# A state-space stage in fp32 on one core: gated output kept in the squares buffer, and six small jobs of VectorE given to GpSimd

## The reference, cut to what matters

```
y = ssd_chunked_scan(x32 * dt[..., None], dt * a_cont, bmat, cmat)
y = y + d_skip[:, None] * x32
y = y.reshape(b, seq, D_INNER) * silu(z)
y = rmsnorm(y.reshape(b, seq, 4, 512), ssd_norm_w.reshape(4, 512))
y_ssd = y.reshape(b, seq, D_INNER) @ w_branch_ssd
# pooling, windows 2, 4, 8, 16
mean = (csg[:, 1:] - start) / minimum(count, float(win))
outs.append(mean - u[..., gi * gw:(gi + 1) * gw])
y_pool = (einsum('blgc,gcd->blgd', pooled, pool_w) * pool_scale) @ w_branch_pool
out = (g_ssd * y_ssd + g_pool * y_pool) @ w_out
```

## Time and profile before

| | |
|---|---|
| Median of 3 runs | 1147.05 us (1146.51 to 1148.46) |
| The profiled execution's own time | 1148.47 us |
| Its span, first to last instruction | 1146.7 us |
| Mean granted TensorE clock | 0.996 |

### The profile page before, as it was taken

One profiled execution on the slowest core, in us unless ns is written; L12 is line 12 of the kernel. 1 busy time (PEld: TensorE's weight loads), 2 busy tenths in 40 slices (PEclk: granted clock), 3 DMA queues, 4 the chain that ended last, 5 costly groups with the idle time before them and its releaser, 6 DMA issues.

```text
span 1146.7 us, 25636 instructions
## 1 busy us (share of the span) xinstructions
PE 1116.8 (97%) x9126; PEld 1076.4 (94%) x9126; DVE 978.8 (85%) x1785; ACT 711.4 (62%) x1109; POOL 34.7 (3%) x64
## 2 busy tenths in 40 slices
PE   8989999999999999999999999999999999999997
PEld 7989999999899999999999989999899999999997
DVE  7877999998998998989999889999997678766667
ACT  6557656666556556565666677878876457645554
POOL 0000000000000100000000000000000000000000
PEclk9999999999999999999999999999999999999999
DMA  8534676675566866856766537457546556665661
GB/s 289 177 119 155 210 238 233 221 262 186 192 251 258 308 225 245 302 198 238 237 209 212 183 101 255 146 202 155 186 155 232 174 197 217 214 198 199 200 202 38
DMA packets 73042, 235.73 MB, mean 206 GB/s; under 512 B 7425, under 2 KB 16641, under 8 KB 72849
## 3 DMA queue, kind: packets, MB, share of 16 engines
q1 hardware_dynamic: 64304, 203.86, 53.4%
q0 software_dynamic: 8528, 30.98, 7.9%
q10 hardware_dynamic: 144, 0.02, 0.0%
HBM read 233.73 MB, written 1.09 MB: 205 GB/s over the span
## 4 chain that ended last, share of the span: by engine, by line
PE 73%; DVE 17%; issue 4%; ACT 4%; DVEq 1%; DMA 1%; ACTq 0%; SPq 0%; another core or an unknown queue 0%
PE ps L248 22%; PE ps L250 21%; PE ps L249 21%; DVE w_lo L240 5%; PE ps L280 3%; PE ps L282 2%; DVE arena L2009 1%; ACT w_hi L235 1%; DVE arena L502 1%; DVE arena L939 1%; DMA w_raw<-stream 1%; DVE arena L1997 0%; PE ps L1674 0%; DVE arena L974 0%; ACT sq L421 0%
## 5 line engine op out<-in xcount | busy, mean ns | idle before, releaser
L240 DVE TENSOR_TENSOR w_lo<-w_raw,w_hi 128x1024 fp32r<-128x1024 f32 x381 | 461.1, 1218 | 11.1 <-ACT w_hi L235 5.1
L248 PE MATMUL ps<-a_hi,w_hi 128*128 128x256 f32 x1656 | 463.8, 280 | 4.8 <-DVE w_lo L240 3.2
L250 PE MATMUL ps<-a_hi,w_lo 128*128 128x256 f32 x1656 | 456.2, 276 | 0.0
L249 PE MATMUL ps<-a_lo,w_hi 128*128 128x256 f32 x1656 | 456.1, 275 | 0.0
L235 ACT ACTIVATE w_hi<-w_raw 128x1024 fp32r<-128x1024 f32 x381 | 390.7, 1049 | 20.9 <-DMA w_raw<-stream 11.8
L248 PEld LDWEIGHTS ps<-a_hi,w_hi 128*128 128x128 f32 x1656 | 318.5, 192 | 12.0 <-issue 5.5
L249 PEld LDWEIGHTS ps<-a_lo,w_hi 128*128 128x128 f32 x1656 | 318.5, 192 | 0.6 <-issue 0.2
L250 PEld LDWEIGHTS ps<-a_hi,w_lo 128*128 128x128 f32 x1656 | 318.7, 192 | 0.0
L248 PE MATMUL ps<-b_both,w_hi 128*128 128x256 f32 x560 | 155.7, 278 | 2.2 <-DVE b_both L999 1.3
L249 PE MATMUL ps<-b_both,w_hi 128*128 128x256 f32 x560 | 154.0, 275 | 0.0
L250 PE MATMUL ps<-b_both,w_lo 128*128 128x256 f32 x560 | 154.0, 275 | 0.0
(11 more groups left out here) (315 smaller groups left out, 1683.1 us busy)
## 6 DMA issues: line engine op xcount, KB each, us to landing
w_raw<-stream SPq DMA_DIRECT2D x381, 512.0 KB, 4.2
arena<-ada POOLq DMA_DIRECT2D x48, 512.0 KB, 5.9
c_both<-cum_rows POOLq DMA_DIRECT2D x4, 1024.0 KB, 8.7
arena<-x SPq DMA_DIRECT2D x2, 512.0 KB, 4.5
con<-consts SPq DMA_DIRECT2D x1, 1024.0 KB, 5.7
arena<-row_cols POOLq DMA_DIRECT2D x2, 512.0 KB, 5.2
arena<-c_rows POOLq DMA_DIRECT2D x1, 512.0 KB, 4.2
out<-arena SPq DMA_DIRECT2D x2, 256.0 KB, 2.2
```

The lines of the kernel that those rows point to most:

```text
L240: dve.tensor_tensor(w_lo[:, s % RING], w_raw[:, s % RING], w_hi[:, s % RING].bitcast(F32), ALU.subtract).then_inc(w_lo_ready, 1)
L248: pe.matmul(o, wh, xh, start=start, stop=False, skip_group_check=shared)
L249: pe.matmul(o, wh, xl, start=False, stop=False, skip_group_check=shared)
L250: return pe.matmul(o, wl, xh, start=False, stop=stop, skip_group_check=shared)
```

## The change

`y_f`, the gated `y`, now lies in `sq[:, 4:8]`. It is written there at j = 0 instead of `z_s` and scaled in place with tokens in order. The even and odd tokens are parted later, when ScalarE copies it to `b_hi` and when the low part is taken. GpSimd gets, in its one queue: for each group the two additions of squares and the low part of `y`, and the low parts of the four poolings (one instruction of 512 columns each instead of two of 256). VectorE waits for the low part of group g - 1 at j = 11 instead of ahead of `gaps(2)`, and from the second pooling on for the low part of the one before. The constant ones for the last pooling's scan move to `sq[:, 3]`, set at m = 5. For the first three groups GpSimd's work stands behind the DMA of the next group's `cum_all`.

```diff
@@ -80,6 +80,11 @@
     return x.rearrange("p m (a t) -> p m a t", a=2)
+def parted_four(x):
+    return x.rearrange("p m (t a) -> p m a t", a=2)
@@ -1530,7 +1535,7 @@
         y_seen = area(4 * SEQ + 2 * SEEN)
-        y_f = y_seen[:, 0:4 * SEQ].rearrange("p (a t) -> p a t", a=4)
+        y_f = sq[:, 4:8]
         seen = [y_seen[:, c:c + SEEN] for c in (4 * SEQ, 4 * SEQ + SEEN, 0, SEEN)]
@@ -1768,13 +1773,13 @@
                     act.wait_ge(yz_ready, in_group(1, 1, g, it))
-                    act.activation(sq[:, 0:4], z_s, ACT.Square).then_inc(ysq_ready, 1)
+                    act.activation(sq[:, 0:4], y_f, ACT.Square).then_inc(ysq_ready, 1)
                 if j == 3:
...
                     o = slice(4 * g, 4 * g + 4) if it is None else bass.ds(it * 4 + 4 * g, 4)
-                    act.activation(b_hi[:, o], y_f, ACT.Copy).then_inc(yhi_ready, 1)
+                    act.activation(halves_wide(b_hi[:, o]), parted_four(y_f), ACT.Copy).then_inc(yhi_ready, 1)
@@ -1903,6 +1908,24 @@
+        def ssd_pool(pool, g):
+            pool.wait_ge(ysq_ready, g + 1)
+            add_four(pool, ADDED_SSD + 2 * g, 2, None)
+            y_low(pool, g)
+        def pooled_lo(pool, g):
+            pool.wait_ge(pooled_hi, g + 1)
+            lo, hi = (halves_wide(x[:, 2 * g:2 * g + 2]) for x in (c_lo, c_hi))
+            pool.tensor_tensor(lo, parted_four(win_of(g)), hi.bitcast(F32), ALU.subtract).then_inc(pooled_operand, 1)
+        def y_low(pool, g):
+            pool.wait_ge(yhi_ready, g + 1)
+            y, hi, lo = parted_four(y_f), halves_wide(b_hi[:, 4 * g:4 * g + 4]), halves_wide(b_lo[:, 4 * g:4 * g + 4])
+            pool.tensor_tensor(lo, y, hi.bitcast(F32), ALU.subtract).then_inc(yssd_ready, 1)
         def win_of(g):
@@ -1958,22 +1981,15 @@
                     dve.wait_ge(z_silu, in_group(1, 1, g, it))
-                    dve.tensor_tensor(z_s, cv[:, 2:6], z_s, ALU.mult).then_inc(yz_ready, 1)
-                if j == 1:
-                    dve.wait_ge(ysq_ready, in_group(1, 1, g, it))
-                    add_four(dve, ADDED_SSD + 2 * g, 2, it)
+                    dve.tensor_tensor(y_f, cv[:, 2:6], z_s, ALU.mult).then_inc(yz_ready, 1)
                 if j == 3:
...
                     for t in range(4):
-                        ins = dve.scalar_tensor_tensor(out=halves(y_f[:, t]), in0=parted(z_s[:, t]), scalar=prm(34 + t, g, it), in1=parted(inv_s),
+                        ins = dve.scalar_tensor_tensor(out=y_f[:, t], in0=y_f[:, t], scalar=prm(34 + t, g, it), in1=inv_s,
                                                        op0=ALU.mult, op1=ALU.mult)
                     ins.then_inc(yn_ready, 1)
-                if j == 7:
-                    dve.wait_ge(yhi_ready, in_group(1, 1, g, it))
-                    o = slice(4 * g, 4 * g + 4) if it is None else bass.ds(it * 4 + 4 * g, 4)
-                    dve.tensor_tensor(b_lo[:, o], y_f, b_hi[:, o].bitcast(F32), ALU.subtract).then_inc(yssd_ready, 1)
@@ -1982,8 +1998,6 @@
                         dve.wait_ge(rows_landed, in_group(16, 16, g, it))
-                    if k == 2 and g:
-                        dve.wait_ge(yssd_ready, in_group(1, 1, g - 1, it))
                     if k >= 4:
@@ -1997,7 +2011,7 @@
                 for j in range(GRP):
-                    if g and j != 7:
+                    if g:
                         tail(j, g - 1, it)
@@ -2029,8 +2043,6 @@
                         weighted(0)
-                    if g and j == 7:
-                        tail(j, g - 1, it)
                     if j > 8:
@@ -2041,6 +2053,8 @@
                         gaps(3)
+                    if g and j == 11:
+                        dve.wait_ge(yssd_ready, in_group(1, 1, g - 1, it))
                     if j == 11:
@@ -2052,7 +2066,6 @@
             dve.wait_ge(u_done, 2 * GROUPS)
-            step(dve.memset(sq[:, NT - 1], 1.0))
@@ -2062,7 +2075,7 @@
                     for t in range(2):
-                        ins = dve.tensor_tensor_scan(running[:, t], sq[:, NT - 1], u[:, t], 0.0, ALU.mult, ALU.add)
+                        ins = dve.tensor_tensor_scan(running[:, t], sq[:, 3], u[:, t], 0.0, ALU.mult, ALU.add)
                     step(ins)
@@ -2078,13 +2091,6 @@
-            def pooled_lo(g):
-                dve.wait_ge(pooled_hi, g + 1)
-                for m in (2 * g, 2 * g + 1):
-                    ins = dve.tensor_tensor(halves(c_lo[:, m]), parted(win_of(g)[:, m % 2]), halves(c_hi[:, m].bitcast(F32)), ALU.subtract)
-                ins.then_inc(pooled_operand, 1)
-                dve.wait_ge(pooled_operand, g + 1)
             def pools():
@@ -2096,14 +2102,15 @@
                 tail(m, GROUPS - 1, None)
-                if m - 1 == POOL_AT[-1]:
-                    pooled_lo(GROUPS - 1)
+                if m == 5:
+                    step(dve.memset(sq[:, 3], 1.0))
                 if m:
...
                 if m in POOL_AT:
-                    pool(POOL_AT.index(m))
-                if m - 1 in POOL_AT and m - 1 != POOL_AT[-1]:
-                    pooled_lo(POOL_AT.index(m - 1))
+                    g = POOL_AT.index(m)
+                    if g:
+                        dve.wait_ge(pooled_operand, g)
+                    pool(g)
             def merge_tile(m, it=None):
@@ -2510,6 +2517,14 @@
                 pool.dma_start(cum_all, cum_rows[g:g + 1].rearrange("a (h t) -> a h t", t=SEQ).broadcast_to((P, GROUP_HEADS, SEQ))).then_inc(rows_landed, 16)
+                if g:
+                    ssd_pool(pool, g - 1)
+            pool.wait_ge(ysq_ready, GROUPS)
+            add_four(pool, ADDED_SSD + 2 * (GROUPS - 1), 2, None)
+            for g in range(GROUPS):
+                pooled_lo(pool, g)
+                if g == 1:
+                    y_low(pool, GROUPS - 1)
             pool.wait_ge(mod_ready, 1)
```

## The result

The changed kernel takes 1150.47 us (median of 20 runs, 1148.33 to 1154.75) beside 1147.11 us (20 runs) of the kernel before: a ratio of 1.003, 95% interval 1.0024 to 1.0037. It is slower by 3.4 us where 5.7 us less were forecast (1141.3 us). The profiled executions differ by 2.65 us (1151.12 against 1148.47).

The account below looks back on a forecast made before the run. VectorE sets the group's 40.40 us, while TensorE needs about 38.0. TensorE waits removed, -7.2 us, plus 1.5 for the disputed price gave -5.7, so 1141.3 us; range 1138.9 to 1150.5, likeliest case 1138.9 to 1142.8.

Parts of the forecast that it names:

- disputed price: VectorE's loss while GpSimd reads the same memory: half of 2.4 us per low part, 1.5 us over three groups.
- slack: Ahead of the head pair, VectorE's remaining lead over TensorE: 0.7 us, absorbing part of the 1.2 us loss.
- rival 1: GpSimd and VectorE lock each other out under two SBUF inputs or two-port modes: 1147.1 to 1149.5 us; chance 0.18.
- rival 2: GpSimd holds VectorE in every job, squares too: 1155.8 us, some 1165 at the high bounds; chance 0.15.
- The additions: Additions of squares on GpSimd: 1.06 us off VectorE per group, 2.25 us on GpSimd, 0.8 us to spare.
- The layout: Scalings of `y` with tokens in order, 424 instead of 512 ns each: 0.35 us less on VectorE per group.
- ScalarE's parted copy: ScalarE's copy with parted tokens: some 0.3 us more, costed at nothing because ScalarE waits often enough.
- The row DMAs: Two small DMAs slip to about 870 us; their rows are used near the end, so costed at nothing.
- 2.7 us from the transposes: TensorE's waits ahead of the transposes fall from 1.6 to 0.5 in two groups, 0.6 to 0 in one.
- 2.3 of the head pairs: TensorE's three waits ahead of a head pair go as VectorE comes 2.54 us earlier: 2.3 us.
- 2.2 for `w_lo`: In the gates VectorE is relieved of over 5 us, so both of TensorE's waits go: 2.2 us.

Follow-up runs that it names:

- h: Changed kernel with the row DMAs at their old early place and GpSimd taking `y`'s low part twice in three groups: 1162.03 us, 1.0123 to the kernel before.
- d: Changed kernel's new layout, but every job back on VectorE at its old place: 1148.51 us, 1.0011 to the kernel before.
- b: As d, with only `y`'s low part on GpSimd: 1151.60 us, 1.0035 to the kernel before.
- c: As d, with only the four poolings' low parts on GpSimd, row DMAs late: 1150.21 us, 1.0023 to the kernel before.
- a: As d, with only the additions of squares on GpSimd: 1146.65 us, 0.9996 to the kernel before.
- l: Kernel before with only the additions of squares moved to GpSimd, old layout: 1146.73 us, 0.9992 to the kernel before.
- f: New layout, only additions on GpSimd, `y`'s low part on VectorE two slabs later, row DMAs early: 1145.90 us, 0.9985 to the kernel before.
- m: As l, with `y_f` in `sq` but still written parted, and the low part late on VectorE: 1146.87 us, 0.9992 to the kernel before.
- j: Kernel before with only the two small row DMAs issued late, near 868 us: 1151.34 us, 1.0033 to the kernel before.
- i: Changed kernel with the two small row DMAs moved back to their old early place: 1149.96 us, 1.0021 to the kernel before.
- n: As c, with the small row DMAs at their old early place: 1149.52 us, 1.0015 to the kernel before.
- e: As i, with GpSimd's low part of `y` held back until gaps 2 and 3 are done: 1149.31 us, 1.0019 to the kernel before.

## Why the prediction was wrong

**The failed step is the disputed price.** The prediction took what VectorE loses while GpSimd reads as half of GpSimd's time, 1.2 us for the low part of `y`, between 0 and the whole. Measured it is 3.17 - 1.00 = 2.17 us per group on four `gaps`, nine tenths of the 2.41 us that GpSimd reads, and h doubles it. 0.7 of it was to vanish in slack; there was none, since VectorE's own chain fills the steady group in the change too: it waits there for nothing but its own results. The steady group shows it in one sum, in us from the measured rows: 40.40 before, less 1.06 for the additions, plus 0.26 for one more gap between dependent taps, less 1.13 for the low part and 0.13 for the scalings, plus 2.17 for the hold makes 40.51; measured 40.47. VectorE comes to the head pair no earlier than before, while TensorE, which waits 0.87 us less for the transposes, comes earlier: 0.77 + 0.87 = 1.64, and its wait is 1.68.

In the gates the same mechanism costs 1.05 us on the scalings, 2.1 on a copy of 4 columns, 1.1 on a `w_lo` twice, and 1.0 and 0.5 on the last two instructions of the first pooling, together 6.9 us against some 5.5 us of work removed, and that work did not set the end everywhere: TensorE's wait for `w_lo` is 2.0 us (2.2 before), and 0.4 for GpSimd's last pooling is new. By the runs the low part costs 3.1 us over d and the poolings 1.7, the late row DMAs in b and c included.

This is the mechanism of rival 1, which had been given 0.18 and 1147.1 to 1149.5; the measured 1150.47 lies 1.0 us above that range. That it lies just inside the prediction's whole range (to 1150.5) is luck: this end was there for the foot of rival 2, which the runs refute. The Trainium skill ("SBUF — State Buffer", Who interferes with whom) has GpSimd and VectorE exclude each other when VectorE's instruction has two SBUF inputs or is in a two-port mode. The trace agrees: `gaps` 3.17 instead of 1.00 us, `w_lo` 2.33 instead of 1.22, and the taps, which read PSUM, not longer beside 2.09 us of additions. The mistake was to read the earlier trace rows (two elements at a time) and this rule side by side and then halve the answer; nothing in the trace spoke for a half. Rival 2, the hold in every job, is refuted for the groups by a and l, and by the taps' usual length; only the last additions, in the gates, held VectorE.

**The additions: right.** They end in time, cost the taps nothing, and take 2.09 us (2.25 taken); the low part takes 2.41 undisturbed (2.4 taken), a pooling 1.30 to 1.92 (1.4). The group shrinks by 0.82 (d to a) and 0.86 (l) instead of 1.06; the difference is about the 0.26 us of the new gap between dependent taps (VectorE waits for its own results 0.3 us per group before, 0.6 in a, l and the change). The transposes' waits fall from 1.6 to 0.7, where 0.5 was forecast. In the first group the gain did not come: from the second to the third `cum_all` DMA it is 41.00 us before and 41.81 in the change (41.72 in a, 40.92 in f). There the wait, forecast gone from 0.6, was 1.0; VectorE waited 0.9 us for ScalarE's copy out of PSUM (L1845) before it could start the taps.

**The layout: far too high.** Costed at -0.35 us per group, it measured +0.41 (d) and +0.45 (l to a) where VectorE takes the low part at j = 7, and about nothing where it takes it at j = 9 (f and m). The mean of 424 ns came from another line whose operands differ; started back to back the four scalings save 0.13. ScalarE's parted copy, costed at nothing for ScalarE "waits often enough", takes 1.36 us instead of 1.04, and in d and a VectorE waits for it; in the change the waiting falls to GpSimd.

**The row DMAs: wrong, but small here.** They were costed at nothing because their rows are due late. What counts is not when they are needed but which weights they meet: 3.7 us in j, 0.5 us (inside the noise) between the change and i, where they delay weights at either place.

**The account of the profiled 2.65 us between the two executions.** The second to fourth `cum_all` DMAs start at 706.60, 747.60 and 788.00 before, at 707.11, 748.92 and 789.39 after. So 0.5 us was lost before the first of the three, ahead of any instruction of the change (GpSimd's first additions start at 716.44); it is not the change's work and stays unexplained. 0.8 is the first group, 0.07 the steady one (less work, more hold), and the remaining 1.3 came behind 789.39: the third tail, the gates and what follows. Forecast for the whole was -5.7: of the 2.7 us from the transposes about 1.4 came, the 2.3 of the head pairs turned into a loss of 2.7 (2.3 to 5.0 us waited), of the 2.2 for `w_lo` 0.2.

**What stays open.** The medians lie 3.4 us apart, the profiled executions 2.65, the fastest runs 1.9 (1146.40 and 1148.33). The changed kernel scatters more, up to 1154.75, and its slowest executions have a mean granted clock of 0.994, the others 0.995 to 0.998. In n's profiled execution a wait of 2.6 us for `w_lo` is followed by a stretch at 0.85 of the clock (866 to 875 us). In i's, which is the changed kernel with the two DMAs back, a wait of 1.90 us for the transposes is followed by 3.3 us at the 1.2 GHz level (from 813.97 us), and in m's likewise; e and f have the same wait without it. So waits of the length that the change has (up to 2.05 us) can cost such a stretch, of some 1.6 us. That this makes the scatter and part of the 3.4 us would fit, but the profile of the changed kernel itself has none, so it is argued and not shown. The parts measured singly add up to 1.2 - 1.9 + 3.1 + 1.7 = 4.1 us against 3.4 for all, within what the intervals allow; a, b and c each have the row DMAs at another place than d, so these are not pure parts.

## What to carry to other kernels

Count GpSimd's elementwise time in full as VectorE's time, wherever VectorE runs instructions with two SBUF inputs or plain single-input fp32 ones; in these runs it was free only where VectorE reads PSUM, and there a job took 0.8 to 0.9 us off a group (a, l). Before moving a job to another engine see whether it can go later on its own: two slabs of delay for the low part took 0.54 us off the group (a to f), and moving it to GpSimd took nothing off (d to b: 0.16 more). A DMA that stands behind moved work in a queue moves with it: see which burst of weights it then meets, above all if it has 4-byte elements.

## What the runs showed of the hardware

- The hold works both ways and is not evenly shared. GpSimd was kept out by consecutive two-input instructions for 4.20 - 2.41 = 1.8 us in e, and longer in c, where a pooling's low part that takes 1.30 undisturbed took 5.09 (timeline of GpSimd in c):

```profile
858.56 5.09 POOL L1919 TENSOR_TENSOR c_both<-arena,c_both 128x512 fp32r<-128x512 f32 x1 [6.79 <-ACT c_both L1883]
```

- Two DMAs of 1,024 elements of 4 bytes keep the 16 DMA engines as busy (0.78) at 120 GB/s as whole weights do at 279 GB/s (0.80), and ScalarE waited up to 9.67 us for a weight slab (c).
- A wait of 3.9 us of TensorE is followed by 4.8 us at the 1.2 GHz level (h). A wait of 1.90 us was followed by 3.3 us at that level in i and m and by none in e and f; the waits of up to 2.05 us in the changed kernel's profile were not.
- ScalarE's copy of 1024 columns takes 1.36 to 1.38 us with every second element read, 1.04 in order. The prediction had expected some 0.3 us more and costed it at nothing.

Not tried: GpSimd instructions that only write, or that read PSUM.
